# Attention heads with scores and masks two pairs ahead, and the division by the row sums on GpSimd

## What is computed

```
scores = q @ k.T * scale          (+ bias or mask)
p      = softmax(scores)          (stage s: with a "sink" logit in the sum)
out    = p @ v
```

## Time and profile before

| | |
|---|---|
| median of 3 runs | 1838.54 us (1837.12 to 1841.63) |
| the profiled execution | 1839.96 us, its span 1838.2 us |
| mean granted TensorE clock | 0.911 of full speed |
| stage a, scores to the last product | about 90 to 130 us |
| stage c | about 478 to 523 us |
| stage s | about 1071 to 1101 us |
| PE, DVE, ACT, POOL busy | 1513.3, 871.4, 591.2, 25.3 us |

### The profile page before, as it was taken

The page is one execution under the profiler, slowest core; times in us unless marked ns, Lnnn a source line. Parts: engine busy times, 40 slices in busy tenths (PEclk is TensorE's granted clock), DMA queues, the critical chain, the costliest instruction groups (busy, mean ns, idle before and its releaser), DMA issues.

```text
span 1838.2 us, 26373 instructions
## 1 busy us (share of the span) xinstructions
PE 1513.3 (82%) x10716; PEld 1217.2 (66%) x10716; DVE 871.4 (47%) x1548; ACT 591.2 (32%) x947; POOL 25.3 (1%) x32
## 2 busy tenths in 40 slices
PE   7876856658677766569998967999999998889997
PEld 6745422226555322249997746999899997769997
DVE  5553211126653211155555686555565555465555
ACT  4351100013441100034433054444344431544442
POOL 0000000001000000000000000000000000000000
PEclk9987988878997987879999978999999998989999
DMA  9502999996123999995554512555545552444520
GB/s 406 213 12 80 375 428 428 429 428 243 46 92 159 427 427 428 429 381 184 188 188 175 169 61 92 196 193 193 196 157 193 193 192 90 173 159 184 183 91 24
DMA packets 31022, 409.21 MB, mean 223 GB/s; under 512 B 3376, under 2 KB 5424, under 8 KB 6368
## 3 DMA queue, kind: packets, MB, share of 16 engines
q1 hardware_dynamic: 28496, 404.85, 55.5%
q10 hardware_dynamic: 2448, 3.24, 0.6%
HBM read 407.02 MB, written 1.06 MB: 222 GB/s over the span
## 4 chain that ended last, share of the span: by engine, by line
PE 56%; DMA 17%; issue 12%; DVE 10%; ACT 4%; POOL 1%; SPq 0%; DVEq 0%; ACTq 0%; POOLq 0%
DMA ring<-stream 17%; PE bank L1359 7%; PE bank L1360 7%; PE bank L1363 7%; PE bank L1391 6%; PE bank L589 5%; PE bank L1397 3%; PE bank L595 3%; PE bank L1632 2%; PE bank L1168 2%; PE bank L1187 2%; PE bank L360 2%; PE bank L569 2%; DVE cat L1576 2%; PE bank L1491 2%
## 5 line engine op out<-in xcount | busy, mean ns | idle before, releaser
L459 DVE TENSOR_TENSOR unit_lo<-ring,unit_hi 128x1024 fp32r<-128x1024 f32 x324 | 395.2, 1225 | 343.7 <-ACT unit_hi L454 343.4
L454 ACT ACTIVATE unit_hi<-ring 128x1024 fp32r<-128x1024 f32 x324 | 341.7, 1060 | 465.7 <-PE bank L1363 285.2
L1359 PE MATMUL bank<-hT_hi,unit_hi 128*128 128x256 f32 x1408 | 342.7, 282 | 0.1
L1360 PE MATMUL bank<-norm_lo,unit_hi 128*128 128x256 f32 x1408 | 341.6, 280 | 0.0
L1359 PEld LDWEIGHTS bank<-hT_hi,unit_hi 128*128 128x128 f32 x1408 | 266.4, 189 | 3.8 <-DVE norm_lo L398 0.5
L1360 PEld LDWEIGHTS bank<-norm_lo,unit_hi 128*128 128x128 f32 x1408 | 265.9, 189 | 3.1
L1168 PE MATMUL bank<-ring,work 128*32 128x256 f32 x2048 | 149.0, 447 | 90.9 <-DMA ring<-stream 78.2
L1363 PE MATMUL bank<-hT_hi,unit_lo 128*128 128x256 f32 x1408 | 194.2, 279 | 0.0
L1168 PEld LDWEIGHTS bank<-ring,work 128*32 128x32 f32 x2048 | 71.3, 125 | 167.9 <-DMA ring<-stream 101.2
L1363 PEld LDWEIGHTS bank<-hT_hi,unit_lo 128*128 128x128 f32 x1408 | 178.1, 188 | 0.0
L1391 PE MATMUL bank<-unit_hi,act_hi 128*128 128x512 f32 x336 | 132.4, 394 | 0.0
(11 more groups left out here) (246 smaller groups left out, 1836.6 us busy)
## 6 DMA issues: line engine op xcount, KB each, us to landing
ring<-stream SPq DMA_DIRECT2D x191, 2048.0 KB, 14.2
work<-spread ACTq DMA_DIRECT2D x2, 1024.0 KB, 7.0
par<-params SPq DMA_DIRECT2D x1, 1455.5 KB, 17.3
x<-x_in SPq DMA_DIRECT2D x1, 1024.0 KB, 4.8
out<-x SPq DMA_DIRECT2D x2, 512.0 KB, 2.7
con<-consts SPq DMA_DIRECT2D x1, 640.0 KB, 5.9
cat<-final_rows ACTq DMA_DIRECT2D x1, 512.0 KB, 3.6
work<-final_rows ACTq DMA_DIRECT2D x1, 512.0 KB, 5.0
```

The costliest lines, as they stand in the source:

```text
L454: nc.scalar.activation(high_buf(name, u), raw_unit(name, u), ACT.Copy).then_inc(hi_done, 1)
L459: low = nc.vector.tensor_tensor(low_buf(name, u), raw_unit(name, u), high_buf(name, u).bitcast(F32), ALU.subtract)
L1359: nc.tensor.matmul(out, high[:, k, :], hT_hi[:, k, :], start=(k == 0), stop=False)
L1360: nc.tensor.matmul(out, high[:, k, :], norm_lo[:, k, :], start=False, stop=False)
```

## The change

It does three things in the attention stages, and nothing elsewhere.

1. PE's scores stand two pairs ahead of the transposes, not one. In a and s they wait for the masks of the pair whose banks they take (`masked_done`), in c as before for its exponential.
2. DVE's masks stand two pairs ahead too: in a and s before the reciprocal of pair i, in c behind it.
3. The four multiplications by the reciprocal go from DVE to GpSimd (`norm_probs_pool`), which waits on a new semaphore `rsum_done`.

```diff
         def scores_pe(pe, name, i):
-            ge(pe, probs_done, g - 1)
+            ge(pe, probs_done if heads[0][4] is None else masked_done, g - 1)
...
             for i in range(n):
-                if i >= 1 and i + 1 < n:
-                    scores_pe(pe, name, i + 1)
+                if i + 2 < n:
+                    scores_pe(pe, name, i + 2)
                 turn_probs_pe(pe, name, i)
...
-        def norm_probs_dve(v, name, i):
+        def sum_probs_dve(v, name, i):
...
-            step(v, nc.vector.reciprocal(rsum, sums))
+            nc.vector.reciprocal(rsum, sums).then_inc(rsum_done, 1)
+
+        def norm_probs_pool(pool, name, i):
+
+            g = PAIR_AT[name] + i
+            pool.wait_ge(rsum_done, g + 1)
+            rsum = pair_stat(g, "rsum")
             for hh in range(2):
                 for t in range(NT):
                     row, c = probs[:, g % 3, hh, t * T:(t + 1) * T], 2 * hh + t
-                    last = nc.vector.tensor_scalar(row, row, rsum[:, c:c + 1], None, ALU.mult)
+                    last = nc.gpsimd.tensor_scalar(row, row, rsum[:, c:c + 1], None, ALU.mult)
             last.then_inc(norm_done, 1)
...
             for i in range(n):
-                norm_probs_dve(v, name, i)
-                if i >= 1 and i + 1 < n:
-                    masked_dve(v, name, i + 1)
+                if i + 2 < n and heads_masked(name):
+                    masked_dve(v, name, i + 2)
+                sum_probs_dve(v, name, i)
+                if i + 2 < n and not heads_masked(name):
+                    masked_dve(v, name, i + 2)
                 if i >= 2:
                     heads_lo_dve(v, name, i - 2)
...
                 power_pool(pool, name, src, dst, w)
+                if name in ("gmlp", "heads", "n5"):
+                    mix = {"gmlp": "a", "heads": "c", "n5": "s"}[name]
+                    for i in range(PAIRS[mix]):
+                        norm_probs_pool(pool, mix, i)
```

More of the change, by code:

```diff
@@ L158, in build @@
         norm_done = sem("norm_done")
+        rsum_done = sem("rsum_done")
         cat_hi, cat_low = sem("cat_hi"), sem("cat_low")
@@ L757, in build, with heads_masked @@
         SINK_NEG = 216
+        def heads_masked(name):
+            return HEADS[name][0][4] is not None
         def pair_stat(g, what):
```

## The result

The changed kernel takes 1876.45 us in the median (1876.01 to 1877.81, 4 runs), the one before 1840.09 us beside it; the ratio is 1.0195, 95% interval 1.0176 to 1.0215. That is 36 us slower, where I had forecast 9 and a range that ended at 1864. The profiled execution has a span of 1875.0 us against 1838.2.

What follows compares the result with a forecast made beforehand. No engine was taken as the bound: chains of waits between engines set the attention stages' time. Terms +12.5 (a), -7.6 (c) and +3.5 (s) sum to +8.4, called +9, giving 1847.5 us; range 1836 to 1864.

Steps and rivals of the forecast that it cites:

- The price d: Time of one 128x256 multiplication on GpSimd: taken as 0.50 us, between bounds of 0.40 and 0.60.
- my own slope of 4.8 us for each 0.1 us: All three stages: per 0.1 us of d, +2.0 us in a, +1.6 in c, +1.2 in s.
- GpSimd becomes the bound: Rival, all stages: a multiplication costs 1.0 us, c gains nothing, a and s lose; +33, 1871 us; chance 0.10.
- The loop is the one forecast: Stage a: transposes, product, scores, masks, reciprocal, GpSimd in turn without overlap; period 7.1 us instead of 5.07, at full clock.
- The clock term: Stage a: PE slows to 1.2 GHz behind 4.0 us idle times, taking +4.9 us at full clock to +12.5.
- The term -7.6: Stage c: a loop through ACT of 6.8 us for two pairs, 3.4 each instead of 4.75, makes it 7.6 us faster.
- +3.5: Stage s: the new loop with only two masks ahead, plus 1.2 us for a collision, makes it 3.5 us slower.
- The collision: Stage s: DVE's multiply-adds with two SBUF inputs hold up GpSimd's multiplications, 0 to 6 us; 1.2 taken.
- The rival built on that rule: Stage s: DVE's multiply-adds lock GpSimd out, +8 us instead of +3.5; 1852 us or more; chance 0.10.
- Slower: Whole kernel: slower by more than 0.3% (5.5 us); chance 0.64.
- theory 2: Set up for the follow-up runs: the new order of the lists alone makes the loss.
- theory 3: Set up for the follow-up runs: the move of the multiplications to GpSimd alone makes the loss.

Runs made afterwards that it cites:

- the one with the copy: Changed kernel with a plain GpSimd copy of each tile onto itself instead of the multiplication, leaving the division out: 1842.01 us, ratio 1.0003 to the kernel before.
- the kernel with the filler: Changed kernel plus 20 extra TensorE transposes, results overwritten, ahead of each pair's transposes in stages a and s: 1866.69 us, ratio 1.0132 to the kernel before.
- the constant: Changed kernel multiplying on GpSimd by a constant instead of a column of SBUF, sums unused: 1871.96 us, ratio 1.0164 to the kernel before.
- the sums first: Changed kernel with reciprocals ahead of the next masks in a and s too: 1841.77 us with GpSimd multiplications, 1816.88 us with copies instead.

## Why the prediction was wrong

**The price d: the step that failed.** I wrote "Together 0.60 us, the upper bound" and took 0.50. That bound was built from the powers' cost with no element and the copies' stream per element, which says that a multiplication streams as a copy does. No row supported that. It measured 0.93 us, 0.91 from start to start. By my own slope of 4.8 us for each 0.1 us this mis-sizing is worth 4.1 x 4.8 = 20 of the 27 us by which I was off (+36 against +9). The slope was too small itself: the changed kernel and the one with the copy differ only in that instruction, 0.93 against 0.40 us, and lie 34 us apart, 6.5 us for each 0.1. A straight line between these two puts a price of 0.50 at about +7.5 (an estimate), near the +9 forecast, so the price can account for the whole miss. The rival "GpSimd becomes the bound" had the price (1.0 us) and the time (1871) nearly right, and a chance of 0.10; my range left it out. Its mechanism did not come: even in stage c GpSimd idled 3.26 of 10.5 us. The powers, at 157 ns an element, were a row that spoke for dear arithmetic, and I set it aside.

**Stage a: right in mechanism.** The loop is the one forecast, in the chain above. With d = 0.91 my terms give 12.5 + 8.2 = +20.7; measured +23.5. The clock term was the right one: 0.78 fell to 0.67, and the transposes behind the idle times of 5.6 us took 1.97 us. One reading behind that term was too simple, though. I had set 1.94 us of idle time, with transposes of 1.09 behind it, against the long ones; the very next pair of the kernel before has as short an idle time and slow work behind it:

```profile
113.81 1.70 PE L785 MATMUL bank<-con,work 128*128 128x128 f32 x8 [1.90 <-DVE work L899]
115.44 1.97 PE L798 MATMUL bank<-work 128*64 128x256 f32 x8
```

The length of the last idle time alone does not tell the clock.

**Stage c: the loop was another at this price.** I had walked it through ACT, 6.8 us for two pairs. At d = 0.91 that would be 8.4; it took 10.5. The rows of the changed kernel show that the reciprocal of pair i+2 was held on DVE by the maxima of pair i+3, and these by the scores behind the product on PE, partly at low clock. I had written "PE idles little here, so the clock should hold"; it fell from 0.96 to 0.82. The term -7.6 became +4.5, of which the price explains 6.6 by my slope and this loop the other 5.5. Of the 2.1 us that a period was longer than 8.4, the low clock made 1.6 (product 1.98 for 1.08, scores 1.84 for 1.13; the period at full clock in the kernel with the filler took 8.90), and the place of the maxima the other 0.5. Where the clock held, my terms held: with the constant (0.82 us from start to start) c was 2.2 us shorter than before at a clock of 0.96, and they give -2.5. With the copy, c gained 9.1, as said. What tips c into the low clock at 0.91 and not at 0.82 is not shown.

**Stage s.** +3.5 and 4.9 for the price make 8.4; measured +10.6. The collision is real and small. Timelines of POOL and DVE:

```profile
1106.24 4.19 POOL L909 TENSOR_SCALAR work<-work,stat 128x256 f32<-128x256 f32 x4 [76.24 <-DVE stat L899]
...
1106.06 2.40 DVE L1588 SCALAR_TENSOR_TENSOR cat<-work,par,cat 128x256 f32<-128x256 f32 x5
1125.47 2.06 DVE L1588 SCALAR_TENSOR_TENSOR cat<-work,par,cat 128x256 f32<-128x256 f32 x5
```

Four multiplications took 4.19 us beside the multiply-adds and 3.63 in stage a with DVE idle; the multiply-adds took 2.40 us beside GpSimd and 2.06 alone. Beside each other GpSimd loses 0.6 us and DVE 0.3. Over the stage the 16 multiplications took 15.9 us instead of 14.5; I had put 1.2 for it. The rule of the Trainium skill (SBUF — State Buffer, section Who interferes with whom) gives the direction that the rows show, but not the size. It has the one that comes second blocked for the whole instruction of the other, and then four multiplications and five multiply-adds would need 3.63 + 2.06 = 5.7 us together; both were done in 4.4 (1106.06 to 1110.43). In the kernel with the copy, four copies took 2.17 us beside the multiply-adds and 1.43 elsewhere. The rival built on that rule, GpSimd locked out for all of the multiply-adds, did not come. In stage a DVE was idle and the price was the same 0.93, so the lock is not what makes the multiplication dear.

**The sign and the pairing of causes.** "Slower" had 0.64 and came. Price and order make each other dearer: with the masks first, the kernel is at 1876 with the multiplication and 1842 with a copy; with the sums first, at 1842 and 1817. Masks first cost 35 us with the multiplication and 25 with the copy; the dear instruction costs 34 us with the masks first and 25 with the sums first. Neither theory 2 nor theory 3 alone accounts for the 36.

## What to carry to other kernels

Before an instruction is put further ahead, write down what it waits for and what stands behind it on its engine: here masks two pairs ahead waited for transposes that waited for a reciprocal behind the next masks, and one line's place was worth 35 us. An operation that the trace does not hold has no upper bound from a cheaper operation on the same engine; the bound needs a row of the same kind of work, or must be left wide. And a loop that leaves TensorE idle must be priced at both clock levels: here the idle times of 5.6 us had the low clock behind them each time, and those of 1.8 to 2.6 us sometimes.

## What the runs showed of the hardware

- GpSimd's `tensor_scalar` in float32 costs about 0.28 us and 2.5 ns an element (128x256 0.93 us, 128x1024 2.88 us), a copy 0.40 us for 128x256 and 1.04 us for 128x1024. A constant in place of the pointer saves 0.08 us.
- Small VectorE instructions can be held while GpSimd multiplies, though most were not. In the attention stages none of 128x4 took over 0.19 us in the kernels where DVE multiplies or GpSimd copies; ten did in four of the six kernels where GpSimd multiplies, among them these two in stage c of the changed kernel, which took twice or more their usual 0.17 us:

```profile
511.01 0.43 DVE L889 TENSOR_SCALAR stat<-stat 128x4 f32<-128x4 f32 x1
511.08 0.35 DVE L899 RECIPROCAL stat<-stat 128x4 f32<-128x4 f32 x1
```
